# Expert blocks of 32 tokens on four column tiles, one store for a block, a second token buffer, and experts ordered by their counts

## The chip, the core and the metric

The kernel runs on one core of a Trainium2 chip. The metric is the device time of one execution in microseconds (us), the median of several runs. The engines named here are PE (TensorE: matmuls, and transposes, which are matmuls against an identity), DVE (VectorE), ACT (ScalarE), POOL (GpSimd) and SP (SyncE, which issues DMAs). ACT and POOL issue DMAs too. Each engine works through its own program in order; they meet through semaphores.

## The reference

One step of a streaming encoder layer with 640 tokens (512 of a prompt, 8 streams of 16) and width 1024, in float32. The change touches its second half, a mixture of 16 experts: a token chooses a group, and in it two experts.

```python
g_sel = jnp.argmax(g_logits, axis=-1)
...
top_v, top_i = lax.top_k(e_in, TOP_K_IN_GROUP)              # 2 of 4 experts of the group
w_sel = jax.nn.softmax(top_v, axis=-1) * g_w
e_ids = g_sel[:, None] * EXPERTS_PER_GROUP + top_i
combine = jnp.sum(jax.nn.one_hot(e_ids, N_EXPERTS) * w_sel[..., None], axis=1)
for e in range(N_EXPERTS):
    h = jax.nn.silu(xt @ lp['w1'][e]) * (xt @ lp['w3'][e])  # (640,1024) @ (1024,512), twice
    y = y + combine[:, e:e + 1] * (h @ lp['w2'][e])         # (640,512) @ (512,1024)
```

So there are 1280 pairs of token and expert. With the inputs of the reference the 16 experts receive 33, 33, 43, 55, 118, 271, 118, 361, 48, 42, 32, 22, 31, 25, 22 and 26 of them.

## The kernel before

The program runs the token mixer first (to about 804 us of the profile), then the routing on DVE and PE (to 819), then the **expert stage** (825.8 to 1160), then a stage that gathers each token's two results, adds them, normalises and stores (to the end).

**Blocks.** In the expert stage the pairs of an expert are cut into blocks of `SLOT` = 64 rows, so the 16 experts have 1, 1, 1, 1, 2, 5, 2, 6 and eight times 1 block, 27 in all, in the order of their numbers. The counts are known only on the chip: `ovc` holds each expert's blocks beyond the first, `ovp` where they start, and every engine reads both into registers (line 1661) at each expert. `each_block` (line 1658) is the loop that all engines share: one step for an expert's first block, whose "down" still belongs to the expert before, and an inner loop (line 1670) for its further blocks.

**A block on PE** (`step`, line 1774). A 64-row block uses half of PE's 128 columns, so two *column tiles* of 64 work side by side, on two halves of the output columns. The order is `up` half 0 (line 1750), `turn_hidden` of the block before (line 1758), `up` half 1, `turn_tokens` of the next block (line 1741), `down` of the block before (line 1769). An `up` half is 8 matmuls of 64 rows by 512 columns (w1 and w3 side by side), a `down` 8 as well. The trace records each of these float32 matmuls as two, so 8 stand there as 16.

**Around it.** POOL gathers the next block's 64 tokens from `xn_scratch` into `xg` with an indirect DMA (line 1716); a token is cut into two pieces, so that the 128 partitions are filled. PE turns `xg` (four transposes), DVE copies them from PSUM to `xe` (line 1832) and then makes the next gather's indices (`idx`, line 1826), on which POOL waits. ACT applies tanh (line 1812) and DVE makes the gated product `gg` in two operations (lines 1844, 1847); `turn_hidden` and a DVE copy give `hT`. After `down`, ACT copies the result from PSUM to `yb` (line 1800) and stores it to `block_outputs` in DRAM with two DMAs of 64 rows of 2 KB (line 1803). Ahead of the copy, ACT waits until the stores of the block before have landed (`y_stored`, line 1798), and PE's `down` waits for the copy of the block before (`y_ready`, line 1763).

**Weights.** An expert has 6 MiB: w1 and w3 in two halves of 2 MiB (rows of 2 KB), w2 of 2 MiB (rows of 4 KB). There are three buffers (`w`, `late` and `on`, in the profile's names). The first three experts' weights are loaded ahead, and SP refills a buffer (`refill`, line 1685) when the last block that reads its part is through: 13 refills.

**The routing** counts on DVE, by comparisons with tables: `over` (16 experts by 10 steps) gives the blocks of each expert, a scan their first rows, and `at_place`/`at_block` are the one-hot matrices from which PE makes the table of indices.

Of the kernel before, what the change touches and what calls it, by code (L numbers as in the profile page):

```python
# [8 lines left out]
I32 = mybir.dt.int32  # L9
# [27 lines left out]
SLOT = 64  # L37
# [5 lines left out]
CREDIT = 1  # L43
GELU_C = float(np.sqrt(2.0 / np.pi))
# [9 lines left out]
K_STEP = K_TOK + TT  # L54
K_PIECE = K_STEP + MAXOV + 1
K_KEEP = K_PIECE + 1
NK = K_KEEP


def shape_constants():  # L60

    c = np.zeros((P, NK + TT * NE), np.float32)
# [12 lines left out]
    c[:, K_STEP + 1:K_STEP + 1 + MAXOV] = SLOT * (1 + np.arange(MAXOV))  # L75
    c[:, K_KEEP:K_KEEP + TT * NE] = np.arange(TT * NE) % TT > 0
    c[:, K_PIECE] = p // SLOT
    c[:, K_DOWN:K_DOWN + 4] = 4 - np.arange(4)
    c[:, K_TOK:K_TOK + TT] = 2 * (p[:, None] + P * np.arange(TT))
    return c  # L80
# [960 lines left out]
def build_rest(nc, A, O, v):  # L1041
# [253 lines left out]
    ovp = sb("ovp", [1, NE + 1], I32)  # L1295
    idxt = sb("idxt", [P, NROWS])
    idx = sb("idx", [P, 1], I32)
    xg = sb("xg", [P, D // 2])
    sm = sb("sm", [P, TT, 16])
    xn2_pieces = xn2_d.rearrange("t (j c) -> (t j) c", j=2)  # L1300
# [56 lines left out]
    keep = sb("keep", [P, TT * NE], ctx=st4)  # L1357
# [5 lines left out]
    over = sb("over", [P, NE, MAXOV + 1], ctx=st4)  # L1363
    nblk = sb("nblk", [P, NE + 1], ctx=st4)
    rowst = sb("rowst", [P, NE + 1], ctx=st4)
# [18 lines left out]
    with nc.Block() as block:  # L1384
        @block.sync
        def _(sp_):
            for t in range(TT):
                if t == 2:
                    sp_.dma_start(wo[1], w_out[:, :, D // 2:]).then_inc(wo_in, 16)
                sp_.dma_start(x2[:, t, :], xp[:, t, :] if t < NQ else xs).then_inc(x2_in[t], 16)  # L1390
            sp_.dma_start(g2[:, :], A["norm2_g"].to_broadcast([P, D])).then_inc(r_in, 16)
            sp_.dma_start(keep[:, :], A["shape_constants"][:, K_KEEP:K_KEEP + TT * NE]).then_inc(r_in, 16)
# [116 lines left out]
        def _(dve):  # L1509
# [70 lines left out]
            nc.vector.tensor_tensor_scan(upto[:, :, :].rearrange("p e t -> p (e t)"), keep[:, :],  # L1580
# [10 lines left out]
            steps = cst[:, K_STEP:K_STEP + MAXOV + 1].rearrange("p (o j) -> p o j", o=1)  # L1591
            tt(over[:, :, :], bank[7][:, TT * NE:(TT + 1) * NE].rearrange("p (e o) -> p e o", o=1)
               .to_broadcast([P, NE, MAXOV + 1]), steps.to_broadcast([P, NE, MAXOV + 1]), ALU.is_gt)
            chain(nc.vector.tensor_reduce(nblk[:, 1:].rearrange("p (e o) -> p e o", o=1), over[:, :, :], AX.X, ALU.add))
            chain(nc.vector.tensor_tensor_scan(rowst[:, :], cst[:, K_ONE:K_ONE + NE + 1], nblk[:, :], 0.0,
                                               ALU.mult, ALU.add))

            rank, row, q, place, slotf = (pr[:, n, :, :] for n in range(5))
            tt(rk[:, :, :, :], oh[:, :, :, :], bank[7][:, 0:TT * NE].rearrange("p (o e t) -> p o t e", o=1, t=TT)
               .to_broadcast([P, 2, TT, NE]), ALU.mult)  # L1600
            nc.vector.tensor_tensor(rk2[:, :, :, :], oh[:, :, :, :], rowst[:, 0:NE].rearrange("p (o i e) -> p o i e", o=1, i=1)
# [8 lines left out]
            for n in range(2 * TT):  # L1610
                k, t = n // TT, n % TT
                nc.vector.tensor_scalar(
                    at_place[:, n, :].rearrange("p (j q) -> p j q", q=SLOT),
                    cst[:, K_RAMP:K_RAMP + SLOT].rearrange("p (o q) -> p o q", o=1).to_broadcast([P, P // SLOT, SLOT]),
                    pr[:, 3, k, t:t + 1], None, ALU.is_equal)
                nc.vector.tensor_scalar(at_block[:, n, :], cst[:, K_RAMP:K_RAMP + NROWS], pr[:, 1, k, t:t + 1],
                                        cst[:, K_TOK + t:K_TOK + t + 1], ALU.is_equal, ALU.mult).then_inc(hot_ready, 1)
            nc.vector.scalar_tensor_tensor(prev[:, :], cst[:, K_RAMP:K_RAMP + NE + 1], -1.0, rowst[:, :], ALU.mult, ALU.add)
# [28 lines left out]
    xt_done, xe_ready = sem("xt_done"), sem("xe_ready")  # L1647
# [34 lines left out]
    with nc.Block() as block:  # L1682
        @block.sync
        def _(sp_):
            def refill(e, buf):

                b = sp_.value_load(ovp[0:1, bass.ds(e - (NBUF - 1), 1)], min_val=0, max_val=OVMAX) + (e - (NBUF - 1))
                for half in range(2):
                    sp_.wait_ge(up_done[half], b)
                    load13(sp_, e, buf, half)  # L1690
                sp_.wait_ge(down_done, b + CREDIT)
                load2(sp_, e, buf)
# [42 lines left out]
        def _(pe):  # L1735
            def turn_tokens(b):
                pe.wait_ge(xg_in, b * 16 + 16)
                if not isinstance(b, int) or b > 0:
                    pe.wait_ge(xe_ready, b)
                for c in range(4):  # L1740
                    mm = nc.tensor.transpose(TOKB[:, c * P:(c + 1) * P], xg[:, c * P:(c + 1) * P], ident)
                mm.then_inc(xt_done, 1)

            def up(S, half):
                buf, n = S.up
                pe.wait_ge(w13_in[half][buf], n * UP_ARRIVED[half][buf])
                for c in range(4):
# [8 lines left out]
            def turn_hidden():  # L1756
                for c in range(2):
                    mm = nc.tensor.transpose(HIDB[:, c * P:(c + 1) * P], gg[:, c * P:(c + 1) * P], ident)  # L1758
                mm.then_inc(ht_done, 1)

            def down(S):
# [33 lines left out]
        def _(act):  # L1795
            def outputs(n, d):

                act.wait_ge(y_stored, n * 32 + (CREDIT - 32))
                act.wait_ge(down_done, d + CREDIT)
                nc.scalar.activation(yb[:, :], DNB[:, :], ACT.Copy).then_inc(y_ready, 1)  # L1800
                act.wait_ge(y_ready, n)
                for x in range(2):
                    act.dma_start(y_d[bass.ds((n - 1) * SLOT, SLOT), x * HD:(x + 1) * HD],
                                  yb[x * SLOT:(x + 1) * SLOT, :]).then_inc(y_stored, 16)
# [9 lines left out]
            def last(S):  # L1814
                outputs(S.b, S.b - 1)
                outputs(S.b + 1, S.b)
                act.wait_ge(y_stored, S.b * 32 + (CREDIT + 32))
# [5 lines left out]
        def _(dve):  # L1823
# [5 lines left out]
            def turned(b):  # L1829

                dve.wait_ge(xt_done, b + 1)
                nc.vector.tensor_copy(xe[:, :, :].rearrange("p c q -> p (c q)"), TOKB[:, :]).then_inc(xe_ready, 1)
                indices(b + 1)

            def hidden(S):
                dve.wait_ge(ht_done, S.b)
                nc.vector.tensor_copy(hT[:, :, :].rearrange("p c q -> p (c q)"), HIDB[:, 0:2 * P]).then_inc(ht_ready, 1)  # L1837

            def step(S):
                if S.down is not None:  # L1840
                    hidden(S)
                turned(S.b + 1)
# [109 lines left out]
```

## Time and profile before

| | us |
|---|---|
| median of 3 runs | 1200.76 (1199.95 to 1201.99) |
| the profiled execution, its own time | 1197.53 |
| its span in the trace | 1195.7 |
| expert stage in it, first `up` to last `down` | 825.8 to 1160.1 |

The span is what the trace covers. The profiled execution lies 0.27% under the median of the runs shown.

### The profile page before, as it was taken

Reading aid. Unit: us, or ns where it says so; the run is one execution under the profiler, and the core shown is the slowest. Engines: PE = TensorE matmul, PEld = TensorE weight load, DVE = VectorE, ACT = ScalarE, POOL = GpSimd, SP = SyncE. Lnnn points to the kernel's source line nnn. Section 1 sums busy time; section 2 is a strip of 40 time slices with the busy share of each in tenths; the row PEclk is TensorE's granted clock in tenths of the full one; section 3 lists DMA queues with packets and bytes.
Section 4 is the critical chain, followed back from the end, with each engine's and each line's share of the span. In section 5 each row is a group of like instructions: output and inputs, shape, how many; then the busy total and the mean of one; then the engine's idle time right before and its main releaser. Section 6 shows DMA issues by size and latency. Waiting matters only on the chain. (4 is left out here: it accounts for less than half of the span.)

```text
span 1195.7 us, 19605 instructions
## 1 busy us (share of the span) xinstructions
PE 1077.0 (90%) x6868; PEld 779.5 (65%) x6869; DVE 498.7 (42%) x979; ACT 266.6 (22%) x584; POOL 420.7 (35%) x461
## 2 busy tenths in 40 slices
PE   3999999999999995999979999986999999999760
PEld 3898888888898884999979994553333333332210
DVE  4448677786868678400051211224111111111106
ACT  4224243242525244311120001210000000000002
POOL 6466382745538300665546640000010110101013
PEclk9999999999999998999989999996999999999895
DMA  7353343242444200522362218917999573489977
GB/s 231 94 152 93 95 129 105 82 115 77 128 112 116 79 15 12 165 70 72 86 219 71 70 40 285 356 62 265 331 397 398 179 280 123 127 305 397 397 257 263
DMA packets 186539, 204.74 MB, mean 171 GB/s; under 512 B 13607, under 2 KB 132391, under 8 KB 186486
## 3 DMA queue, kind: packets, MB, share of 16 engines
q1 hardware_dynamic: 174790, 177.79, 45.0%
q10 hardware_dynamic: 7936, 13.37, 3.4%
q0 software_dynamic: 3760, 12.85, 3.1%
q8 instruction: 36, 0.59, 0.2%
q14 instruction: 17, 0.14, 0.0%
HBM read 180.84 MB, written 22.95 MB: 170 GB/s over the span
## 5 line engine op out<-in xcount | busy, mean ns | idle before, releaser
L178 POOL TENSOR_TENSOR wh<-raw,zcol 128x256 fp32r<-128x256 f32 x160 | 112.5, 703 | 173.4 <-DMA raw<-in_w_in 164.6
L1750 PE MATMUL bank<-w,xe 128*64 128x512 f32 x576 | 134.7, 611 | 12.2 <-DMA w<-in_w 9.6
L181 POOL TENSOR_TENSOR wl<-raw,wh 128x256 fp32r<-128x256 f32 x160 | 126.9, 793 | 12.6
L493 PE MATMUL bank<-xh,wh 128*128 128x320 f32 x384 | 122.3, 318 | 0.0
L494 PE MATMUL bank<-xl,wh 128*128 128x320 f32 x384 | 118.7, 309 | 0.0
L495 PE MATMUL bank<-xh,wl 128*128 128x320 f32 x384 | 118.7, 309 | 0.0
L1722 POOL TENSOR_TENSOR gate<-gate 128x1 f32<-128x1 f32 x27 | 5.2, 193 | 285.5 <-DVE idx L1826 282.8
L493 PE MATMUL bank<-wh,xh 128*128 128x256 f32 x320 | 93.6, 293 | 7.1 <-POOL wl L181 7.1
L1750 PEld LDWEIGHTS bank<-w,xe 128*64 128x64 f32 x576 | 40.4, 140 | 91.0 <-issue 78.0
L1153 POOL TENSOR_TENSOR w3h<-wraw,zcol 128x1024 fp32r<-128x1024 f32 x32 | 60.9, 1903 | 87.8 <-PE bank L1196 84.0
L494 PE MATMUL bank<-wl,xh 128*128 128x256 f32 x320 | 90.4, 283 | 0.0
L495 PE MATMUL bank<-wh,xl 128*128 128x256 f32 x320 | 90.4, 282 | 0.0
L1194 PE MATMUL bank<-bh,w3h 128*128 128x320 f32 x256 | 79.9, 312 | 6.1 <-DVE bl L1276 6.1
L1157 POOL TENSOR_TENSOR w3l<-wraw,w3h 128x1024 fp32r<-128x1024 f32 x32 | 80.9, 2529 | 2.5
L1837 DVE COPY hT<-bank 128x256 f32<-128x256 f32 x27 | 11.5, 424 | 165.5 <-PE bank L1758 165.5
L1195 PE MATMUL bank<-bl,w3h 128*128 128x320 f32 x256 | 79.6, 311 | 0.0
L1196 PE MATMUL bank<-bh,w3l 128*128 128x320 f32 x256 | 79.6, 311 | 0.0
L1194 PE MATMUL bank<-xh,w3h 128*128 128x320 f32 x256 | 79.1, 309 | 0.0
L493 PEld LDWEIGHTS bank<-xh,wh 128*128 128x128 f32 x384 | 72.1, 188 | 10.5 <-issue 10.5
L1196 PE MATMUL bank<-xh,w3l 128*128 128x320 f32 x256 | 79.0, 308 | 0.0
L1195 PE MATMUL bank<-xl,w3h 128*128 128x320 f32 x256 | 78.9, 308 | 0.0
L494 PEld LDWEIGHTS bank<-xl,wh 128*128 128x128 f32 x384 | 72.2, 188 | 0.2 <-issue 0.2
(273 smaller groups left out, 2076.5 us busy)
## 6 DMA issues: line engine op xcount, KB each, us to landing
w<-in_w SPq DMA_DIRECT2D x44, 1024.0 KB, 15.7
w<-in_w SPq DMA_DIRECT2D x11, 2048.0 KB, 17.7
raw<-in_w_in SPq DMA_DIRECT2D x38, 512.0 KB, 5.0
late<-in_w SPq DMA_DIRECT2D x10, 1024.0 KB
on<-in_w SPq DMA_DIRECT2D x5, 2048.0 KB, 15.5
kc<-in_cache_k SPq DMA_DIRECT2D x8, 1024.0 KB, 6.9
vc<-in_cache_v SPq DMA_DIRECT2D x8, 1024.0 KB, 6.1
wraw<-in_w_in SPq DMA_DIRECT2D x16, 512.0 KB, 4.0
```

The costliest lines, as they stand in the source:

```text
L178: nc.gpsimd.tensor_tensor(wh[:, k, j, :], r[:, k, :], zcol[:, 0:1].rearrange("p (a b) -> p a b", a=1) .to_broadcast([P, KT // PIECES, P]), ...
L181: ins = nc.gpsimd.tensor_tensor(wl[:, k, j, :], r[:, k, :], wh[:, k, j, :].bitcast(F32), ALU.subtract)
L493: nc.tensor.matmul(out, ah, bh, start=(k == 0), stop=False)
L494: nc.tensor.matmul(out, ah, bl, start=False, stop=False)
L495: mm = nc.tensor.matmul(out, al, bh, start=False, stop=(k == len(pairs) - 1))
L1153: nc.gpsimd.tensor_tensor(w3h[j][:, :, :], wraw[j][:, :, :], zcol3[:, 0:1].rearrange("p (a b) -> p a b", a=1).to_broadcast([P, KT, P]), AL ...
L1157: nc.gpsimd.tensor_tensor(w3l[j][:, :, :], wraw[j][:, :, :], w3h[j][:, :, :].bitcast(F32), ALU.subtract).then_inc(w3_split, 1)
L1194: nc.tensor.matmul(out, w3h[j][:, k, :], mh[:, k, c], start=(k == 0), stop=False)
L1195: nc.tensor.matmul(out, w3h[j][:, k, :], ml[:, k, c], start=False, stop=False)
L1196: mm = nc.tensor.matmul(out, w3l[j][:, k, :], mh[:, k, c], start=False, stop=(k == KT - 1))
L1750: mm = nc.tensor.matmul(UPB[j * SLOT:(j + 1) * SLOT, :], xe[:, c, half * SLOT:(half + 1) * SLOT], up_rows(buf, k, k + 1)[:, 0, :, j * HF:( ...
L1837: nc.vector.tensor_copy(hT[:, :, :].rearrange("p c q -> p (c q)"), HIDB[:, 0:2 * P]).then_inc(ht_ready, 1)
```

## The change

Blocks have `SLOT` = 32 rows, so the experts have 2, 2, 2, 2, 4, 9, 4, 12, 2, 2 and six times 1 block, 47 in all. PE works in four column tiles of 32: an `up` half and a `down` are 16 matmuls of 32 rows by 256 columns. A token is cut into four pieces of 256, `xg` is 128 x 256, `turn_tokens` has two transposes and `turn_hidden` one.

The gathered tokens go from `xg` to a second buffer, `xs`, by a DVE copy (`staged`) that stands ahead of the copy of the turned tokens; the indices for the next gather, and that gather, no longer wait for the transposes but for this copy.

A block's result leaves `yb` (128 partitions of 256) in one DMA: its DRAM side is written as 4 pieces by 32 rows by 256 columns, its SBUF side as 128 partitions.

The experts come in another order: `FIXED` = 3 stay first, the others are ranked by their counts and `SPREAD` says which rank comes at which turn. By the counts above the experts come as 0, 1, 2, 7, 14, 11, 5, 13, 15, 4, 12, 10, 6, 9, 8, 3, with 2, 2, 2, 12, 1, 1, 9, 1, 1, 4, 1, 1, 4, 2, 2, 2 blocks. DVE makes that order in the routing, and SP reads from a table (`turn_of`) which expert's weights to load.

```diff
-SLOT = 64
+SLOT = 32
+NP = P // SLOT
...
+FIXED = 3
+SPREAD = (0, 1, 2, 3, 15, 14, 4, 13, 12, 5, 11, 10, 6, 9, 8, 7)
...
+    c[:, K_KEY:K_KEY + NE] = np.where(e < FIXED, 4096.0 * (FIXED - e), -e / 32.0)
+    c[:, K_RANK:K_RANK + NE] = SPREAD
...
+            tt(key[:, :], counts, late_k[:, K_KEY - NK:K_RANK - NK], ALU.add)
+            tt(larger[:, :, :], key[:, :].rearrange("p (o e) -> p o e", o=1).to_broadcast(pairs),
+               key[:, :].rearrange("p (e o) -> p e o", o=1).to_broadcast(pairs), ALU.is_gt)
+            nc.vector.tensor_reduce(rank_e[:, :].rearrange("p (e o) -> p e o", o=1), larger[:, :, :], AX.X, ALU.add)
...
+            tt(at_turn[:, :, :], rank_e[:, :].rearrange("p (o e) -> p o e", o=1).to_broadcast(pairs),
+               late_k[:, K_RANK - NK:NK4 - NK].rearrange("p (i o) -> p i o", o=1).to_broadcast(pairs), ALU.is_equal)
...
                 b = sp_.value_load(ovp[0:1, bass.ds(e - (NBUF - 1), 1)], min_val=0, max_val=OVMAX) + (e - (NBUF - 1))
+                x = sp_.value_load(turn_of[0:1, bass.ds(e, 1)], min_val=0, max_val=NE - 1)
                 for half in range(2):
                     sp_.wait_ge(up_done[half], b)
-                    load13(sp_, e, buf, half)
+                    load13(sp_, x, buf, half)
...
             def gather(b):
-                if not isinstance(b, int) or b > 0:
-                    pool.wait_ge(xt_done, b)
+                pool.wait_ge(xs_ready, b)
                 pool.wait_ge(idx_in, b + 1)
...
-                for c in range(4):
-                    k = half * 4 + c
-                    for j in range(2):
-                        mm = nc.tensor.matmul(UPB[j * SLOT:(j + 1) * SLOT, :],
-                                              xe[:, c, half * SLOT:(half + 1) * SLOT],
+                for k in range(half * KT // 2, (half + 1) * KT // 2):
+                    x, c = k // XC, k % XC
+                    for j in range(NP):
+                        mm = nc.tensor.matmul(UPB[j * SLOT:(j + 1) * SLOT, 0:2 * HF],
+                                              xe[:, c, x * SLOT:(x + 1) * SLOT],
                                               up_rows(buf, k, k + 1)[:, 0, :, j * HF:(j + 1) * HF],
                                               start=(k == 0), stop=(k == KT - 1))
...
-                act.wait_ge(y_stored, n * 32 + (CREDIT - 32))
+                act.wait_ge(y_stored, n * 16 + (CREDIT - 16))
                 act.wait_ge(down_done, d + CREDIT)
-                nc.scalar.activation(yb[:, :], DNB[:, :], ACT.Copy).then_inc(y_ready, 1)
+                nc.scalar.activation(yb[:, :], DNB[:, 0:HD], ACT.Copy).then_inc(y_ready, 1)
                 act.wait_ge(y_ready, n)
-                for x in range(2):
-                    act.dma_start(y_d[bass.ds((n - 1) * SLOT, SLOT), x * HD:(x + 1) * HD],
-                                  yb[x * SLOT:(x + 1) * SLOT, :]).then_inc(y_stored, 16)
+                act.dma_start(y_d[bass.ds((n - 1) * SLOT, SLOT), :].rearrange("s (x c) -> x s c", x=NP), yb[:, :]) \
+                    .then_inc(y_stored, 16)
...
+            def staged(b):
+
+                dve.wait_ge(xg_in, b * 16 + 16)
+                if not isinstance(b, int) or b > 0:
+                    dve.wait_ge(xt_done, b)
+                nc.vector.tensor_copy(xs[:, :], xg[:, :]).then_inc(xs_ready, 1)
                 indices(b + 1)
...
                 if S.down is not None:
                     hidden(S)
+                staged(S.b + 1)
                 turned(S.b + 1)
```

The first piece of the program's order is PE's, before the change, from an expert's first block (whose `down` reads `w_1`) into the inner loop; REGISTER_ALU, TENSOR_LOAD, ISA and the branches are work of PE's sequencer.

```order
L1750 MATMUL bank<-late,xe 64x512 x8
L1737 ISA
L1741 MATMUL bank<-cst,xg 128x128 x4
L1769 MATMUL bank<-w_1,hT 64x512 x8
L1661 REGISTER_ALU
L1661 TENSOR_LOAD ovc
L1661 ISA x2
L1669 COMPARE_AND_BRANCH
L1661 TENSOR_LOAD ovp
```

The same place of PE's program after the change:

```order
L1788 MATMUL bank<-late,xe 32x256 x16
L1775 REGISTER_ALU
L1779 MATMUL bank<-cst,xs 128x128 x2
L1804 MATMUL bank<-w_1,hT 32x256 x16
L1699 REGISTER_ALU
L1699 TENSOR_LOAD ovc
L1699 ISA x2
L1707 COMPARE_AND_BRANCH
L1699 TENSOR_LOAD ovp
```

The register work stands in the same place with the same rows, behind a `down` of 16 small matmuls instead of 8 large ones. The second place is ACT's inner loop; before the change (the brackets name the semaphores that an instruction waits for):

```order
L1800 ACTIVATE yb<-bank 128x512 [waits down_done,y_stored]
L1803 ISA [waits y_ready]
L1803 DMA block_outputs<-yb 64x512
L1803 ISA
L1803 DMA block_outputs<-yb 64x512
L1809 REGISTER_ALU
L1812 ACTIVATE th<-bank 128x256 [waits s_ready,up_done1]
```

And after it:

```order
L1835 ACTIVATE yb<-bank 128x256 [waits down_done,y_stored]
L1837 ISA [waits y_ready]
L1837 DMA block_outputs<-yb 4x32x256
L1843 REGISTER_ALU
L1846 ACTIVATE th<-bank 128x128 [waits s_ready,up_done1]
```

One DMA whose outermost count is 4 has taken the place of two whose outermost count is 64; the copy still waits for the store before it, and the tanh stands behind both. The third place is DVE's inner loop after the change:

```order
L1878 COPY hT<-bank 128x128 [waits ht_done]
L1870 ISA
L1873 COPY xs<-xg 128x256 [waits xt_done,xg_in]
L1860 ISA
L1860 TENSOR_SCALAR idx<-idxt 128x1
L1865 REGISTER_ALU
L1866 COPY xe<-bank 128x256 [waits xt_done]
L1886 SCALAR_TENSOR_TENSOR gg<-th,bank 128x128 [waits th_ready]
L1889 SCALAR_TENSOR_TENSOR gg<-gg,bank 128x128 [waits s_ready]
```

Before, DVE had no copy from `xg` and made `idx` behind the copy to `xe`; the wait for the gather (`xg_in`) has moved from PE's transposes to DVE, ahead of `xe` and `gg`.

## Rows read from the trace of the kernel before

**Rows 1.** Stretches: length, busy PE, PEld, DVE, ACT, POOL, PE clock, DMA share, GB/s

```profile
826.00:1160.00 334.00, 317.06 (x1458) 105.80 (x1458) 52.78 (x140) 26.46 (x54) 32.09 (x55) 0.99 0.79 290
...
1104.00:1117.00 13.00, 9.74 (x34) 2.88 (x34) 0.42 (x1) 0.00 (x0) 0.00 (x0) 0.74 1.04 398
```

**Rows 2.** Timeline of one block of 64 tokens, PE and ACT

```profile
883.53 0.60 ACT L1800 ACTIVATE yb<-bank 128x512 f32<-128x512 f32 x1 [3.85 <-PE bank L1769]
...
887.15 3.65 PE L1750 MATMUL bank<-w,xe 128*64 128x512 f32 x16
...
890.74 0.66 PE L1741 MATMUL bank<-cst,xg 128*128 128x128 f32 x4
...
891.33 3.65 PE L1769 MATMUL bank<-w,hT 128*64 128x512 f32 x16
...
895.09 0.60 ACT L1800 ACTIVATE yb<-bank 128x512 f32<-128x512 f32 x1 [3.85 <-PE bank L1769]
...
895.86 1.19 ACTq L1803 DMA_DIRECT2D block_outputs<-yb  x2
```

**Rows 3.** Timeline of TensorE, an attention line on four column tiles

```profile
57.00 1.07 PE L582 MATMUL bank<-kc,qbd 128*32 128x256 f32 x16 [0.44 <-ACT kc L713]
```

**Rows 4.** Line 1661 between two one-block experts, 1052.5 to 1055.6

```profile
L1661 PEldq TENSOR_LOAD <-ovc x1: 307/307/307, 1053.2 to 1053.2; - x1
...
L1661 PEldq TENSOR_LOAD <-ovp x1: 305/305/305, 1054.3 to 1054.3; - x1
```

**Rows 5.** Line 1746 in the same stretch

```profile
L1746 PEldq FUSED_REGOPS  x1: 37/37/37, 1055.2 to 1055.2; - x1
```

**Rows 6.** Timeline of TensorE in that stretch

```profile
1053.12 3.65 PE L1769 MATMUL bank<-w,hT 128*64 128x512 f32 x16
```

**Rows 7.** Waits of TensorE in the stage: total, times, longest

```profile
PE bank L1750 <- DMA w<-in_w: 9.6, 4, 4.0
PE bank L1750 <- DMA late<-in_w: 4.9, 2, 2.6
```

**Rows 8.** Timeline of TensorE after its longest wait

```profile
1107.26 6.16 PE L1750 MATMUL bank<-w,xe 128*64 128x512 f32 x16 [3.99 <-DMA w<-in_w]
```

**Rows 9.** Timeline of SyncE's DMA issues, w2 of four late refills

```profile
1083.29 2.56 SPq L1338 DMA_DIRECT2D w<-in_w  x1
...
1134.92 2.47 SPq L1338 DMA_DIRECT2D w<-in_w  x1
```

**Rows 10.** All stores of the stage, issue to landing

```profile
DMA to landing us min/median/max: 2.3/5.4/7.4
```

**Rows 11.** Packets, MB, share of 16 engines by queue, 872.7 to 878.3

```profile
q1 hardware_dynamic: 723, 1.67, 78.2%
q10 hardware_dynamic: 144, 0.25, 12.0%
```

**Rows 12.** DMA traffic of line 1138's stores, 699.2 to 701.2

```profile
DMA packets 60, 0.15 MB, mean 74 GB/s; under 512 B 24, under 2 KB 24, under 8 KB 60
...
out_new_conv_sample<-srow SPq DMA_DIRECT2D x1, 96.0 KB
```

**Rows 13.** Gathers into xg, issue to landing

```profile
DMA to landing us min/median/max: 3.0/6.0/7.8
```

**Rows 14.** Timeline of VectorE in the routing

```profile
811.38 0.32 DVE L1513 TENSOR_TENSOR rk<-oh,bank 128x160 f32<-128x160 f32 x1
811.74 0.32 DVE L1601 TENSOR_TENSOR rk<-oh,rowst 128x160 f32<-128x160 f32 x1
...
818.67 0.26 DVE L1624 TENSOR_SCALAR idxt<-bank,cst 128x38 f32<-128x38 f32 x1 [0.49 <-PE bank L1468]
```

**Rows 15.** Timeline of TensorE at the stage's first block

```profile
825.82 8.67 PE L1750 MATMUL bank<-w,xe 128*64 128x512 f32 x32 [0.78 <-DVE xe L1832]
```

**Rows 16.** Timeline at the stage's end

```profile
1161.00 1.13 ACTq L1803 DMA_DIRECT2D block_outputs<-yb  x2
1163.94 0.20 ACT L1818 ACTIVATE gate<-eps_t 128x1 f32<-128x1 f32 x1 [3.12 <-DMA block_outputs<-yb]
```

More of the change, by code:

```diff
@@ L53 @@
 K_ID, K_ONE, K_UPTO, K_SEL, K_M0, K_M1, K_RAMP, K_DOWN, K_TOK = (0, 128, 256, 384, 448, 449, 450, 578, 582)
[L54 to L57, printed above, removed]
+K_PIECE = K_TOK + TT
+NK = K_PIECE + 1
+K_KEEP = NK
+K_STEP = K_KEEP + TT * NE
+K_KEY = K_STEP + MAXOV + 1
+K_RANK = K_KEY + NE
+NK4 = K_RANK + NE
 def shape_constants():
-    c = np.zeros((P, NK + TT * NE), np.float32)
+    c = np.zeros((P, NK4), np.float32)
     p = np.arange(P)
@@ L1356, in build_rest @@
     gap = sb("gap", [P, TT, NG], ctx=st4)
-    keep = sb("keep", [P, TT * NE], ctx=st4)
+    late_k = sb("late_k", [P, NK4 - NK], ctx=st4)
+    keep = late_k[:, 0:TT * NE]
     oh = sb("oh", [P, 2, TT, NE], ctx=st4)
@@ L1362, in build_rest @@
     rk2 = sb("rk2", [P, 2, TT, NE], ctx=st4)
-    over = sb("over", [P, NE, MAXOV + 1], ctx=st4)
+    over = x2T[:, 4:, :].rearrange("p k q -> p (k q)")[:, 0:NE * (MAXOV + 1)].rearrange("p (e o) -> p e o", e=NE)
     nblk = sb("nblk", [P, NE + 1], ctx=st4)
+    nblk_e = sb("nblk_e", [P, NE], ctx=st4)
+    key = sb("key", [P, NE], ctx=st4)
+    larger, at_turn = (x2T[:, 2 * i:2 * i + 2, :].rearrange("p k q -> p (k q)").rearrange("p (a b) -> p a b", b=NE)
+                       for i in range(2))
+    rank_e = sb("rank_e", [P, NE], ctx=st4)
+    rowst_e = sb("rowst_e", [P, NE], ctx=st4)
+    who = sb("who", [P, NE], ctx=st4)
     rowst = sb("rowst", [P, NE + 1], ctx=st4)
@@ L1391, in _ @@
             sp_.dma_start(g2[:, :], A["norm2_g"].to_broadcast([P, D])).then_inc(r_in, 16)
-            sp_.dma_start(keep[:, :], A["shape_constants"][:, K_KEEP:K_KEEP + TT * NE]).then_inc(r_in, 16)
+            sp_.dma_start(late_k[:, :], A["shape_constants"][:, NK:NK4]).then_inc(r_in, 16)
             sp_.dma_start(wr[:, :, 0:NG], A["w_group"][0].rearrange("(k p) n -> p k n", p=P)).then_inc(r_in, 16)
@@ L1579, in _ @@
             dve.wait_ge(oh_ready, 1)
-            nc.vector.tensor_tensor_scan(upto[:, :, :].rearrange("p e t -> p (e t)"), keep[:, :],
+            nc.vector.tensor_tensor_scan(upto[:, :, :].rearrange("p e t -> p (e t)"), keep,
                                          both[:, :, :].rearrange("p e t -> p (e t)"), 0.0, ALU.mult, ALU.add) \
@@ L1590, in _ @@
             dve.wait_ge(ranks_done, 1)
-            steps = cst[:, K_STEP:K_STEP + MAXOV + 1].rearrange("p (o j) -> p o j", o=1)
+            steps = late_k[:, K_STEP - NK:K_KEY - NK].rearrange("p (o j) -> p o j", o=1)
+            counts = bank[7][:, TT * NE:(TT + 1) * NE]
+            pairs = [P, NE, NE]
+            tt(key[:, :], counts, late_k[:, K_KEY - NK:K_RANK - NK], ALU.add)
+            tt(larger[:, :, :], key[:, :].rearrange("p (o e) -> p o e", o=1).to_broadcast(pairs),
+               key[:, :].rearrange("p (e o) -> p e o", o=1).to_broadcast(pairs), ALU.is_gt)
+            nc.vector.tensor_reduce(rank_e[:, :].rearrange("p (e o) -> p e o", o=1), larger[:, :, :], AX.X, ALU.add)
             tt(over[:, :, :], bank[7][:, TT * NE:(TT + 1) * NE].rearrange("p (e o) -> p e o", o=1)
                .to_broadcast([P, NE, MAXOV + 1]), steps.to_broadcast([P, NE, MAXOV + 1]), ALU.is_gt)
-            chain(nc.vector.tensor_reduce(nblk[:, 1:].rearrange("p (e o) -> p e o", o=1), over[:, :, :], AX.X, ALU.add))
+            nc.vector.tensor_reduce(nblk_e[:, :].rearrange("p (e o) -> p e o", o=1), over[:, :, :], AX.X, ALU.add)
+            tt(at_turn[:, :, :], rank_e[:, :].rearrange("p (o e) -> p o e", o=1).to_broadcast(pairs),
+               late_k[:, K_RANK - NK:NK4 - NK].rearrange("p (i o) -> p i o", o=1).to_broadcast(pairs), ALU.is_equal)
+            tt(larger[:, :, :], at_turn[:, :, :], nblk_e[:, :].rearrange("p (o e) -> p o e", o=1).to_broadcast(pairs),
+               ALU.mult)
+            chain(nc.vector.tensor_reduce(nblk[:, 1:].rearrange("p (i o) -> p i o", o=1), larger[:, :, :], AX.X, ALU.add))
             chain(nc.vector.tensor_tensor_scan(rowst[:, :], cst[:, K_ONE:K_ONE + NE + 1], nblk[:, :], 0.0,
                                                ALU.mult, ALU.add))
+            tt(larger[:, :, :], at_turn[:, :, :].rearrange("p i e -> p e i"),
+               rowst[:, 0:NE].rearrange("p (o i) -> p o i", o=1).to_broadcast(pairs), ALU.mult)
+            nc.vector.tensor_reduce(rowst_e[:, :].rearrange("p (e o) -> p e o", o=1), larger[:, :, :], AX.X, ALU.add)
             rank, row, q, place, slotf = (pr[:, n, :, :] for n in range(5))
@@ L1617, in _ @@
                                         cst[:, K_TOK + t:K_TOK + t + 1], ALU.is_equal, ALU.mult).then_inc(hot_ready, 1)
+            tt(larger[:, :, :], at_turn[:, :, :],
+               cst[:, K_RAMP:K_RAMP + NE].rearrange("p (o e) -> p o e", o=1).to_broadcast(pairs), ALU.mult)
+            chain(nc.vector.tensor_reduce(who[:, :].rearrange("p (i o) -> p i o", o=1), larger[:, :, :], AX.X, ALU.add))
+            nc.vector.tensor_copy(turn_of[:, :], who[0:1, :])
             nc.vector.scalar_tensor_tensor(prev[:, :], cst[:, K_RAMP:K_RAMP + NE + 1], -1.0, rowst[:, :], ALU.mult, ALU.add)
@@ L1736, in turn_tokens @@
             def turn_tokens(b):
-                pe.wait_ge(xg_in, b * 16 + 16)
+                pe.wait_ge(xs_ready, b + 1)
                 if not isinstance(b, int) or b > 0:
                     pe.wait_ge(xe_ready, b)
-                for c in range(4):
-                    mm = nc.tensor.transpose(TOKB[:, c * P:(c + 1) * P], xg[:, c * P:(c + 1) * P], ident)
+                for c in range(XC):
+                    mm = nc.tensor.transpose(TOKB[:, c * P:(c + 1) * P], xs[:, c * P:(c + 1) * P], ident)
                 mm.then_inc(xt_done, 1)
@@ L1756, in turn_hidden @@
             def turn_hidden():
-                for c in range(2):
-                    mm = nc.tensor.transpose(HIDB[:, c * P:(c + 1) * P], gg[:, c * P:(c + 1) * P], ident)
-                mm.then_inc(ht_done, 1)
+                nc.tensor.transpose(HIDB[:, 0:P], gg[:, :], ident).then_inc(ht_done, 1)
             def down(S):
@@ L1766, in down @@
                 for k in range(DNC):
-                    j, c = k // 2, k % 2
-                    for x in range(2):
-                        mm = nc.tensor.matmul(DNB[x * SLOT:(x + 1) * SLOT, :], hT[:, c, j * SLOT:(j + 1) * SLOT],
+                    for x in range(NP):
+                        mm = nc.tensor.matmul(DNB[x * SLOT:(x + 1) * SLOT, 0:HD], hT[:, k * SLOT:(k + 1) * SLOT],
                                               w2b[buf][:, k, x * HD:(x + 1) * HD],
```

32 lines of the change are left out of this document (17 added, 15 removed).

## The prediction

> **What bounds it now.** I read the stretches first: of the 334.00 us of the expert stage PE is busy 317.06, at a granted clock of 0.99 [rows 1]. So this stage goes at PE's pace, and the timeline of a block shows the pace: an `up` half at 887.15, the token transposes at 890.74 and `down` at 891.33 follow one another without a wait, and ACT's copies to `yb`, one a block, start at 883.53 and 895.09, 11.56 us apart [rows 2]. An `up` half, eight pairs of column tiles, takes 3.59 to the next piece: 0.43 a pair and 0.15 of transition. 24 pairs are 10.3 us of a block, the transitions 1.25. The list of waits shows where PE stands still: 9.6 + 4.9 = 14.5 us, all for weights, at the end of the stage [rows 7]. After the longest of these waits, 3.99 us, an `up` half took 6.16 instead of 3.65 [rows 8], and the granted clock of that stretch is 0.74 [rows 1]: 2.5 us more. ACT, DVE, POOL and the stores are hidden today: the loaded landing of a store, 5.4 us in the median [rows 10], fits into a block of 11.56. That cover is what I watch, because the change halves it.
>
> **Matmuls on four column tiles.** 256 columns instead of 512 make a step of four tiles 0.43/2 = 0.215 us. The nearest row agrees: 16 recorded matmuls of 128 x 256 on tiles of 32, four steps, took 1.07 us with the last one's tail [rows 3], where two tiles at a time would need eight steps, 1.7. A block is then 24 x 0.215 = 5.17, plus transitions of 0.90 (three transposes fewer): 6.07. 47 blocks are 285.3 us, against 27 x 11.556 = 312.0 today: **-26.7**.
>
> **Register work between experts.** At 1053 to 1055, between two one-block experts, PE's sequencer reads `ovc` at 1053.2 and `ovp` at 1054.3 (0.31 each) [rows 4] and comes to the next `up` at 1055.2 [rows 5], 2.1 us after the first of it. `down` had begun at 1053.12 [rows 6]: the sequencer pushes `down`'s 16 pairs and runs ahead of them, so today 3.5 us of matmuls hide the 2.1. After the change the same 16 pairs are half a `down`, about 0.86 us. I charge the difference, 1.3 us, at six one-block experts (7.8). Entering an inner loop has three register loads, some 0.6 more: 1.9 at ten experts (19); leaving one has one load: 0.5 to 1.05 at nine (6.7). Together **+33.5**. Bounds: 12 if the queue holds all 32 pairs of the new `down`, 45 if it holds fewer than 16.
>
> **Weights.** The late waits come from eight one-block experts in a row, for which 11.56 us do not cover a refill: `w2` refills are issued at 1083.29 and, three later, at 1134.92, 17.2 us each [rows 9]. In the new order the blocks of 12, 9, 4 and 4 stand between groups of small experts. I keep 4 of the 17 (14.5 + 2.5): **-13**.
>
> **Routing.** `over` doubles to 320 elements, and nine operations of up to 256 elements are new ahead of the one-hot matrices or behind them. Operations of 160 elements start 0.36 apart (811.38, 811.74), so I take 0.45 for 256; the 0.49 that DVE waits before `idxt` hides a part [rows 14]: +4.2. At the first block the copy to `xs` adds 0.4; two transposes fewer and a smaller `xe` copy give 0.8 back. First `up` at 829.6 instead of 825.82 [rows 15]: **+3.8**.
>
> **Gather.** It may start earlier, but must land within a 6.07 us block; it takes 3.0 to 7.8, 6.0 in the median [rows 13]. With 0.9 of copy and issue around it, it binds only in inner loops under loads: +2 (0 to 5), in the 4 kept above. The wait stands on DVE now: behind it are `idx`, `xe` and `gg`, and PE's transposes and next `up` wait for those.
>
> **The store.** Two issues become one, which saves ACT some 0.6 a block, hidden either way; at the very end the second issue and half the copy fall away, -0.85. But the shape of the one DMA changes how many DMA engines carry it. The state stores of line 1138 show how: they have 3, 24, 1 and 8 rows, and their traffic is 60 packets, 36 rows and 24 small completion writes [rows 12]. 24 is 3 + 12 + 1 + 8: not 16 for the 24-row store, but 12, the largest number up to 16 that divides its outermost count. Today's 64 rows give 16 engines with four 2 KB rows each. The new store is 128 partitions on one side and 4 pieces x 32 x 256 on the other. No store before has two sides that differ, but to be cut alike on both by the outermost count it has four parts: four engines with 32 rows of 1 KB each. The Trainium skill, page "DMA: Bandwidth & Descriptors", section "Why a DMA increments its semaphore by 16 and not by 1", states the rule for both patterns, which would be four here; the 24 writes agree for equal sides, and no run here shows unequal ones.
>
> Its price: while a store landed under loads, 128 store rows took 12.0% of 16 engines over 5.6 us, 84 ns each, and 723 packets of the weights' queue 78.2%, 97 ns each [rows 11]. A 1 KB row is 42 ns, and one weight row comes between two store rows: 28 further rows x 0.139 = 3.9, on top of 5.4: landing after 9.3 us. Bounds: 6.6 if the rows go without alternating (28 x 0.042), 11.3 behind 4 KB weight rows (28 x 0.210). Idle: 2.3 + 1.2 = 3.5.
>
> ACT's next copy waits for that landing, behind it stands the tanh, and PE's `down` waits for the copy. A block under loads then takes 0.38 (copy) + 0.17 (895.69 to the issue at 895.86 [rows 2]) + 9.3 + 0.1 = 9.95, instead of 6.07 + 33.5/47 = 6.78: 3.2 more. Loads last 13 x 17.2 = 224 us, and the four engines carry 24 KB more a block, at 393 KB per 17.2 us another 1.05: n = (224 + 1.05 n)/9.95, n = 25. I take 22, since a store issued near a load's end lands in a quiet DMA: 22 x 3.2 = **+70**. The waits kept above hide behind it, -3.
>
> **The sum.** The stage ends today at 1160.1: 825.8 + 312.0 + 1.4 (first halves at a low clock, 8.67 [rows 15]) + 17 + 3.3 (first and last block's helpers) = 1159.5. After: 829.6 + 285.3 + 1.5 + 33.5 + 4 + 2 = 1156; with the four-engine store 1156 + 67 = 1223. From stage end to the finished execution is 1197.5 - 1160.1 = 37.4; the last store costs 1.2 more landing less 0.85 (today 1161.00 to 1163.94 [rows 16]). 1223 + 37.4 + 0.3 = 1261 in the profiled execution's time; the median of the runs stood 3.2 above that: **1264 us**, 5% slower.
>
> **The rivals.**
> - *The store runs on 16 engines* (the 128 partitions decide). It then lands within 5.4 to 6.1, hidden, and the sum is 1156 + 37.4 - 0.85 = 1192.6, median **1196**: faster. The change decides for gain where a store lands in under about 6 us.
> - *The same, and PE's queue holds the whole `down`.* Register stalls 12 instead of 33.5: about **1176**. Against it: the sequencer goes on just when `down`'s first matmul starts [rows 4, 6], so the rows show it 16 pairs ahead, not 32.
> - *Four engines, rows not alternating.* Landing 6.6, period 7.25, 0.5 more for 31 blocks: **1212**.
> - *Four engines and the clock falls.* The 3.9 us that PE waits per block come in one piece at `down`, as long as the 3.99 that took the clock away. A half-clock block is up to 12.1 us, 2.2 above the period: +48 at most, **1310**. For it: the one case of [rows 8]; against it: the 2.5 us of a slower half disappear in the same slack, and the clock would have to stay down through all loaded blocks.
> - *Column tiles of 32 do not overlap* would cost hundreds of us; the attention line excludes it.
>
> **Numbers.** Four engines as worked out, 1225 to 1303: 0.56; with a lost clock above that, 0.06; without alternation, 1200 to 1225: 0.14. Sixteen engines: 0.24, of which a third at 1176 to 1187. A difference of 0.2% (2.4 us) is about what the runs can tell from none. Faster 0.20, same 0.05, slower 0.75. The range 1192 to 1303 leaves out some 0.13 below and 0.06 above; four engines alone, 1205 to 1303.
>
> **What would show it.** The landing of `block_outputs`: about 9 us under loads and 3.5 idle, or 5.4 and 2.3 if wrong; DMA traffic of a lone store with four completion writes, not 16; ACT's `yb` copies waiting for `block_outputs`, PE's `down` for `yb`, blocks of 10 us under loads and 6.1 without. Steps of PE: four tiles every 0.215; sequencer gaps of 1 to 2 us between experts and none inside loops; weight waits under 4 us in all; `idxt` 4 us later. Short landings with PE busy throughout would make the prediction wrong.

## The result, and the profile after

The changed kernel takes 1241.98 us (median of 4 runs, 1240.91 to 1245.09) against 1201.38 for the kernel before (4 runs): a ratio of 1.0335, interval 1.0314 to 1.0356. It is slower by 3.4%; forecast were 1264 us and 5%. Its profiled execution took 1242.42, its span is 1240.7.

The stretch of the expert stage, in the columns of [rows 1]:

```profile
829.90:1204.00 374.10, 311.30 (x4654) 160.02 (x4653) 73.12 (x289) 31.11 (x94) 55.07 (x95) 0.94 0.69 254
```

The stage lasts from 830.5 to 1203.4: 372.9 us, where it was 334.3. PE is busy for 311 of it, hardly less than before, and the mean granted clock is 0.94 instead of 0.99. The lists of waits say where the rest goes. First PE (total, times, longest), then ACT; "issue" stands for a gap in which the engine waited for nothing that the profile shows. Line 1788 is an `up` half, 1804 `down`, 1779 the token transposes, 1835 the copy to `yb`, 1846 the tanh, 1889 the end of `gg`, 1873 the copy to `xs`:

```profile
PE bank L1804 <- ACT yb L1835: 46.2, 23, 3.3
PE bank L1788 <- DVE gg L1889: 7.6, 10, 1.3
PE bank L1788 <- issue: 7.6, 12, 1.3
PE bank L1779 <- DVE xs L1873: 3.7, 1, 3.7
...
```

```profile
ACT yb L1835 <- DMA block_outputs<-yb: 193.7, 28, 8.4
ACT th L1846 <- PE bank L1788: 98.4, 24, 24.4
ACT yb L1835 <- PE bank L1804: 36.4, 18, 2.1
...
```

The 3.7 us for `xs` lie ahead of the first `up`. No wait for weights is left; the 14.5 us of [rows 7] are gone. In their place `down` (line 1804) waits 46.2 us for the copy to `yb`, 23 times, and that copy stood still for 193.7 us because the store ahead of it had not landed. The timeline of ACT and PE in a stretch with weight loads shows one turn of it:

```profile
853.71 0.39 ACT L1835 ACTIVATE yb<-bank 128x256 f32<-128x256 f32 x1 [5.64 <-DMA block_outputs<-yb]
854.29 1.06 ACTq L1837 DMA_DIRECT2D block_outputs<-yb  x1
...
864.20 0.38 ACT L1835 ACTIVATE yb<-bank 128x256 f32<-128x256 f32 x1 [8.35 <-DMA block_outputs<-yb]
...
864.63 3.59 PE L1804 MATMUL bank<-w,hT 128*32 128x256 f32 x32 [2.64 <-ACT yb L1835]
864.76 1.05 ACTq L1837 DMA_DIRECT2D block_outputs<-yb  x1
...
873.27 0.38 ACT L1835 ACTIVATE yb<-bank 128x256 f32<-128x256 f32 x1 [7.00 <-DMA block_outputs<-yb]
...
873.71 1.93 PE L1804 MATMUL bank<-on,hT 128*32 128x256 f32 x32 [1.08 <-ACT yb L1835]
```

The copy at 853.71 is stored from 854.29 on; the next copy starts at 864.20, as soon as that store has landed, 9.9 us after its issue, and the one after that at 873.27, 8.5 after the issue at 864.76. The copies were 11.56 us apart for 64 rows [rows 2]; here they are 9 to 10.5 apart for 32. After the wait of 2.64 us one `down` took 3.59 us instead of 1.93; the stretch of that `down` and the next `up` half, in the columns of [rows 1]:

```profile
864.60:868.20 3.60, 3.57 (x32) 1.41 (x33) 0.57 (x2) 0.28 (x1) 0.00 (x0) 0.53 1.04 383
868.20:870.10 1.90, 1.90 (x37) 1.13 (x33) 0.00 (x0) 0.00 (x0) 0.00 (x0) 1.00 0.98 344
```

The granted clock is 0.53 in the first, about the lower of its two levels (1.2 instead of 2.4 GHz), and 1.00 in the second. Between the weight loads the same program does what its matmuls allow:

```profile
1024.01 0.39 ACT L1835 ACTIVATE yb<-bank 128x256 f32<-128x256 f32 x1 [2.02 <-PE bank L1804]
1024.57 0.56 ACTq L1837 DMA_DIRECT2D block_outputs<-yb  x1
...
1030.09 0.38 ACT L1835 ACTIVATE yb<-bank 128x256 f32<-128x256 f32 x1 [2.02 <-PE bank L1804]
```

Copies are 6.08 us apart there, and ACT waits for PE, no longer for the DMA. The last store lands in an otherwise quiet DMA, so its traffic can be counted as in [rows 12]:

```profile
DMA packets 132, 0.13 MB, mean 41 GB/s; under 512 B 4, under 2 KB 132, under 8 KB 132
...
q10 hardware_dynamic: 132, 0.13, 13.8%
...
block_outputs<-yb ACTq DMA_DIRECT2D x1, 128.0 KB
```

132 packets are 128 rows of 1 KB and 4 completion writes: four DMA engines. The same count at the end of the kernel before:

```profile
DMA packets 160, 0.26 MB, mean 90 GB/s; under 512 B 32, under 2 KB 32, under 8 KB 160
```

Its two stores together have 160 packets, 128 rows and 32 writes, 16 for each.

### The profile page after: what moved, and what is told of

The parts are those of the page before. It is cut to its first block and busy times, and to the rows that moved or that the text cites. A ratio compares the mean times of both kernels' runs of the same rounds, so it can differ in the third digit from the quotient of the medians.

```text
span 1240.7 us, 27023 instructions
## 1 busy us (share of the span) xinstructions
PE 1070.9 (86%) x10061; PEld 833.0 (67%) x10062; DVE 520.9 (42%) x1138; ACT 271.5 (22%) x624; POOL 442.7 (36%) x501
## 5 line engine op out<-in xcount | busy, mean ns | idle before, releaser
L1788 PE MATMUL bank<-w,xe 128*32 128x256 f32 x2560 | 159.4, 391 | 13.9 <-DVE gg L1889 7.0
L1788 PEld LDWEIGHTS bank<-w,xe 128*32 128x32 f32 x2560 | 81.3, 112 | 76.1 <-issue 29.7
L1804 PE MATMUL bank<-w,hT 128*32 128x256 f32 x1280 | 87.5, 420 | 35.4 <-ACT yb L1835 35.3
L1760 POOL TENSOR_TENSOR gate<-gate 128x1 f32<-128x1 f32 x47 | 9.1, 193 | 292.3 <-DVE idx L1860 290.5
L1804 PEld LDWEIGHTS bank<-w,hT 128*32 128x32 f32 x1280 | 41.3, 119 | 68.6 <-issue 42.4
L502 PEld LDWEIGHTS bank<-xh,wh 128*128 128x128 f32 x384 | 72.0, 188 | 10.5 <-issue 10.2
```

The costliest lines, as they stand in the source:

```text
L502: nc.tensor.matmul(out, ah, bh, start=(k == 0), stop=False)
L1788: mm = nc.tensor.matmul(UPB[j * SLOT:(j + 1) * SLOT, 0:2 * HF], xe[:, c, x * SLOT:(x + 1) * SLOT], up_rows(buf, k, k + 1)[:, 0, :, j * HF: ...
L1804: mm = nc.tensor.matmul(DNB[x * SLOT:(x + 1) * SLOT, 0:HD], hT[:, k * SLOT:(k + 1) * SLOT], w2b[buf][:, k, x * HD:(x + 1) * HD], start=(k ...
```

## The experiments

All times are medians, and the ratios, with 95% intervals, are to the kernel before in runs on the same chip. The theory was that the one store runs on four engines, that it lands late under weight loads, and that ACT's wait for it sets the pace; the main rivals were the register work between experts, blocks of 32 rows as such, and the load that the stores put on four engines.

| kernel | us | ratio (interval) |
|---|---|---|
| the change | 1241.98 | 1.0335 (1.0314 to 1.0356) |
| `two_engines`: the store as two, on two engines | 1307.91 | 1.0874 (1.0836 to 1.0912) |
| `before_one_store`: before, its two stores as one | 1281.60 | 1.0681 (1.0640 to 1.0722) |
| `own_order`: the change, experts by number | 1249.13 | 1.0401 (1.0373 to 1.0429) |
| `four_stores`: the change with four stores a block | 1196.22 | 0.9953 (0.9936 to 0.9970) |
| `four_own_order`: that, experts by number | 1218.78 | 1.0140 (1.0119 to 1.0160) |
| `four_one_buffer`: that, without the second token buffer | 1206.19 | 1.0032 (1.0016 to 1.0048) |
| `four_reads`: that, register reads moved | 1191.90 | 0.9916 (0.9899 to 0.9933) |
| `two_buffers`: the change, two result buffers | 1207.22 | 1.0047 (1.0030 to 1.0065) |
| `two_buffers_reads`: that, register reads moved | 1207.71 | 1.0051 (1.0030 to 1.0072) |
| `before_order`: before, with the order alone | 1186.14 | 0.9872 (0.9850 to 0.9894) |

**Four stores.** One store for each piece of 32 rows, as the two stores before.

```diff
...
-                act.dma_start(y_d[bass.ds((n - 1) * SLOT, SLOT), :].rearrange("s (x c) -> x s c", x=NP), yb[:, :]) \
-                    .then_inc(y_stored, 16)
+                for x in range(NP):
+                    act.dma_start(y_d[bass.ds((n - 1) * SLOT, SLOT), x * HD:(x + 1) * HD],
+                                  yb[x * SLOT:(x + 1) * SLOT, :]).then_inc(y_stored, 16)
```

> The changed kernel with its one store cut into four again, one for each 32 rows of 1 KB. Theory (the single store runs on four DMA engines, and the next copy waits for its landing): both sides of each DMA are 32 rows, so 16 engines carry it; landing under loads 5 to 6 us, ACT's wait for it small, the 46.2 us that PE waits for the copies and most of the 14 us at a low clock behind them go: 1242 - 55 = about 1185 us, 1178 to 1195. Rival (32-row blocks as such are too short for any store under loads, or the four issues of 0.5 us each load ACT): PE keeps at least half of its waits, 1215 or more.

1196.22 us, 46 less than the change. The DMA traffic of one block's four stores, and PE's waits in the stage:

```profile
DMA packets 192, 0.13 MB, mean 35 GB/s; under 512 B 64, under 2 KB 192, under 8 KB 192
```

```profile
PE bank L1788 <- issue: 12.6, 16, 1.3
PE bank L1788 <- DVE gg L1890: 8.3, 7, 1.8
PE bank L1788 <- DMA w<-in_w: 6.9, 2, 3.9
PE bank L1779 <- DVE xs L1874: 6.4, 7, 3.7
...
PE bank L1804 <- ACT yb L1835: 0.4, 1, 0.4
```

128 rows now have 64 completion writes, four times 16. PE's wait for the copies has shrunk from 46.2 us to 0.4. The theory holds; the size expected was 11 us too good, and the time lies just outside its range, because other waits come up behind it: for weights (6.9 after none), ahead of `up` with no cause shown (12.6 after 7.6), and for the second token buffer (2.7 of the 6.4; the other 3.7 lie ahead of the first `up`, as in the change). The prediction's first rival had 1196 for just this case, though its terms for the weights and the register work were others.

**More rows on fewer engines.** The store as two DMAs of 2 pieces by 32 rows each, and, on the kernel before, its two stores joined into one of 2 pieces by 64 rows:

```diff
...
+                for h in range(2):
+                    act.dma_start(y_d[bass.ds((n - 1) * SLOT, SLOT), h * 2 * HD:(h + 1) * 2 * HD]
+                                  .rearrange("s (x c) -> x s c", x=2),
+                                  yb[h * 2 * SLOT:(h + 1) * 2 * SLOT, :]).then_inc(y_stored, 16)
```

> The changed kernel with its store cut into two DMAs of 2 pieces by 32 rows. Theory: each runs on two engines, and both on the same two, so these carry 64 rows each instead of 32; 32 more rows at 0.2 us under loads are 6.4 us: landing 15 to 16, blocks under loads 16.5, some 14 to 16 of them: 1290 to 1320 us. Rival (the number of engines is not what makes the landing long): two issues instead of one cost at most 0.5 us a block on ACT: 1242 to 1255.

```diff
-                for x in range(2):
-                    act.dma_start(y_d[bass.ds((n - 1) * SLOT, SLOT), x * HD:(x + 1) * HD],
-                                  yb[x * SLOT:(x + 1) * SLOT, :]).then_inc(y_stored, 16)
+                act.dma_start(y_d[bass.ds((n - 1) * SLOT, SLOT), :].rearrange("s (x c) -> x s c", x=2), yb[:, :]) \
+                    .then_inc(y_stored, 16)
```

> The kernel before with nothing changed but its two stores joined into one DMA of 2 pieces by 64 rows of 2 KB. Theory: two engines with 64 rows each, at 0.084 + 0.097 us a row under loads 11.6 us on top of 4: landing about 16, longer than its block of 11.56: some 14 blocks under loads cost 5 us more, 1255 to 1290 us. Rival (a block of 64 rows covers it, or one issue less helps): 1196 to 1204.

1307.91 and 1281.60 us, both inside what the theory gave and far from the rivals. The waits of PE and ACT in the first, then ACT's and the last store's traffic in the second:

```profile
PE bank L1804 <- ACT yb L1835: 95.4, 19, 8.9
```

```profile
ACT yb L1835 <- DMA block_outputs<-yb: 243.2, 32, 13.8
```

```profile
ACT yb L1800 <- DMA block_outputs<-yb: 224.9, 20, 16.7
```

```profile
DMA packets 130, 0.26 MB, mean 32 GB/s; under 512 B 2, under 2 KB 2, under 8 KB 130
```

With half the engines PE's wait doubles (46.2 to 95.4 us), and ACT's longest wait goes from 8.4 to 13.8 us. That the two stores of a block share the same two engines is read from this, not counted. In the joined store, with 64 rows of 2 KB an engine, it is 16.7, where the kernel before had no such wait; of the 80 us that this kernel is slower, PE's waits for the copy are 35.1 (35.7 after 0.6), its waits for weights 16.1 (30.6 after 14.5), and matmuls at a low clock some 18. Without weight loads the last store lands 3.3 us after its issue in the change, 5.0 in `two_engines`, and 7.9 joined. The joined store has 128 rows and 2 completion writes: the outermost count of its DRAM side is 2. So the smaller of the two sides' counts decides, in both kernels, and no block size is needed to make it costly.

**The wait or the load.** The one store stays, but `yb` has two halves with a semaphore each, so a copy waits for the store before the last.

```diff
+                def put(i):
+                    act.wait_ge(y_stored[i], (n + i) * 8)
...
+                with act.If(n % 2 == 0):
+                    put(0)
+                with act.Else():
+                    put(1)
```

> The changed kernel, its one store on four engines left as it is, with two result buffers and a semaphore for each (ACT branches on the block's parity): a copy waits for the store before the last. Theory (the price is the wait for the landing, 8 to 10 us against a block of 6.1): two blocks of 6.1 cover it, PE's 46 us of waits for copies and the 14 us of low clock go: 1185 to 1200 us. Rival (the price is the load on four DMA engines: store rows hold up the weights' rows there): weights come late instead, 1210 to 1235.

1207.22 us: 35 us of the 46 come back, 11 do not. The expectation was missed on its upper side, and the rival's on its lower. ACT's copies never wait for a store now, PE's waits are others; behind them the landing of `w2`, issue to landing, in the saturated stretch 1040 to 1140, here and with four stores:

```profile
PE bank L1789 <- issue: 15.6, 18, 1.3
PE bank L1789 <- DMA w<-in_w: 14.3, 3, 8.8
...
PE bank L1789 <- DMA late<-in_w: 3.3, 1, 3.3
```

```profile
DMA to landing us min/median/max: 18.6/19.4/21.1
```

```profile
DMA to landing us min/median/max: 17.5/17.6/18.2
```

A `w2` load needs 19.4 us instead of 17.6, and PE waits 14.3 + 3.3 us for weights instead of 6.9. So three quarters of the loss was the wait. For the last quarter the 10.7 us more of waits for weights speak for the load on four engines, which the wait had hidden as long as it held the blocks up; no run takes that load away alone, and the branch on the block's parity, which is new here, may have a part in it ("issue" 15.6 after 12.6).

**Register reads.** An expert's three reads are moved into its first block's step, on PE behind the hidden transpose, the second `up` half and the token transposes, first on the kernel with four stores (there on ACT too, behind its store), then on the one with two buffers.

```diff
+                S.read()
                 up(S, 1)
+                S.read()
                 turn_tokens(S.b + 1)
+                S.read()
```

> The kernel with four stores a block, and on PE and ACT an expert's three register reads moved from behind its first block's step into it (PE: behind the hidden transpose, behind the second up half, behind the token transposes). Theory (the 27 us that PE stands still between a down and the next up, beyond 0.2 a block, are mostly the sequencer reading registers with only about 16 pairs ahead): 10 to 16 of them go, 1180 to 1187 us. Rival (the tanh, late behind four store issues, ends these gaps): 1192 to 1198.

> The same with PE's register reads moved into the first block's step. Theory: with one store issue instead of four the tanh is not late, so more of the register gaps is kept than the 4 us which the kernel with four stores gave: 6 to 12 us below the kernel with two buffers, 1175 to 1192. Rival (the gathers and weights take up what the reads give): within 4 us of it.

1191.90 us, 4 less than the kernel with four stores and just under the rival's range, and 1207.71, no gain, as the rival had it. PE's waits with four stores:

```profile
PE bank L1788 <- DVE xs L1888: 9.2, 11, 3.7
PE bank L1797 <- DVE gg L1904: 6.0, 6, 2.3
PE bank L1797 <- DMA w<-in_w: 5.9, 2, 4.3
PE bank L1813 <- issue: 5.2, 12, 0.6
PE bank L1797 <- issue: 1.0, 4, 0.3
...
```

The gaps ahead of `up` with no other cause ("issue") have gone from 12.6 to 1.0 us, so the register reads did make them. But 5.2 of it comes back ahead of `down`, and the gathers take more (9.2 after 6.4). With two buffers "issue" goes from 15.6 to 5.6 us (4.5 of it ahead of `down`), the waits for the gathered tokens inside the stage from 5.4 to 13.5, and those for weights stay (17.6 and 17.7). Both expectations of a large gain were wrong: what is freed runs into the gather.

**The order of the experts.** With the tables set to the order of the numbers, once with the one store and once with four:

```diff
-FIXED = 3
-SPREAD = (0, 1, 2, 3, 15, 14, 4, 13, 12, 5, 11, 10, 6, 9, 8, 7)
+FIXED = NE
+SPREAD = tuple(range(NE))
```

> The changed kernel with the experts in the order of their numbers (the tables alone differ; the routing's operations stay). Theory of the order: six one-block experts stand together at the end, each needs 17 to 18 us for its weights and some 10 us for its block, so PE waits 5 to 8 us for weights six times: 1270 to 1290 us. Rival (the order is worth nothing while the stores set the pace): 1240 to 1250.

> The kernel with four stores a block and the experts in the order of their numbers. Theory of the order: the six one-block experts at the end need about 17 us of weights each and have 7.5 us of work; part of the loads runs ahead, some 20 to 35 us of waits are left: 1212 to 1232 us. Rival (with short blocks the loads are the bound in any order): 1193 to 1202.

1249.13 and 1218.78 us. The order is worth 7 us in the change and 23 us with four stores. Of PE's waits in the first:

```profile
PE bank L1804 <- ACT yb L1835: 30.8, 16, 3.3
PE bank L1788 <- DMA w<-in_w: 11.4, 4, 5.4
PE bank L1788 <- DMA late<-in_w: 8.8, 2, 6.4
```

And for weights in the second:

```profile
PE bank L1788 <- DMA w<-in_w: 19.3, 5, 7.3
...
PE bank L1788 <- DMA late<-in_w: 8.8, 2, 7.1
```

28.1 us, against 6.9 in the new order. With one store the first expectation was too high, and its rival's range held: PE waits 20.2 us for weights there, but its waits for the copy are 30.8 us instead of 46.2. Then the order alone, on the kernel before (of the change's diff the tables, the routing, `turn_of` and SP's read of it):

```diff
 SLOT = 64
+NP = P // SLOT
...
+FIXED = 3
+SPREAD = (0, 1, 2, 3, 15, 14, 4, 13, 12, 5, 11, 10, 6, 9, 8, 7)
...
+                x = sp_.value_load(turn_of[0:1, bass.ds(e, 1)], min_val=0, max_val=NE - 1)
```

> The kernel before with the new order of the experts alone: blocks of 64 rows, two stores, one token buffer as they were. Theory (the order spreads the large experts, so PE's 14.5 us of weight waits and the 2.5 us of low clock go, but for some 3 us; the new routing operations cost 3.7): 1202 - 17 + 3 + 3.7, 1187 to 1195 us. Rival (runs of two one-block experts at 11.6 us against 17.2 us of weights still wait, and the routing eats the rest): 1198 to 1206.

1186.14 us, the fastest of all, 1 below the range expected. All waits that the list has for PE (the first lies ahead of the stage's first `up`):

```profile
PE bank L1779 <- PEq L1402: 3.9, 1, 3.9
PE bank L1788 <- DVE gg L1885: 1.9, 1, 1.9
PE bank L1788 <- DVE xe L1870: 0.8, 1, 0.8
PE bank L1807 <- ACT yb L1838: 0.6, 1, 0.6
```

Not one for weights; the stage is 317.5 us long, 16.8 less than before, which is the 14.5 + 2.5 us of [rows 7, 8].

**The second token buffer.** With four stores, PE turns `xg` itself again, and the indices come behind `xe`.

```diff
-                pe.wait_ge(xs_ready, b + 1)
+                pe.wait_ge(xg_in, b * 16 + 16)
...
-                staged(S.b + 1)
                 turned(S.b + 1)
+                staged(S.b + 1)
```

> The kernel with four stores a block and without the second token buffer: PE turns the gathered tokens from where they land, as before. Theory: the next gather starts 1.6 us behind the token transposes instead of 0.4 ahead, needs 5.6 us under loads and a block lasts 6.1: 1 to 1.5 us more in each loaded block that stands in a loop, none without loads: 1208 to 1230 us. Rival (the gather hides in a block either way): 1193 to 1198.

1206.19 us: 10 more than with four stores, a little less than the theory gave (12 was its least) and far from the rival. PE's wait for the gather:

```profile
PE bank L1780 <- DMA xg<-xn_scratch,idx: 20.6, 17, 2.9
```

20.6 us where it was 2.7 inside the stage with the buffer. A block of 6.1 us needs the buffer.

## Why the prediction came out as it did

**The direction and its cause were right.** The store's engines follow the outermost counts of both sides: four writes in 132 packets, two in the joined store of the kernel before. ACT's wait for the landing and PE's wait behind it are what the change cost; taking them away gives 46 us back (four stores), doubling the rows on each engine costs 66 more, 49 of it in waits and 18 in matmuls at a low clock. The Trainium skill, page "DMA: Bandwidth & Descriptors", section "Why a DMA increments its semaphore by 16 and not by 1", takes the largest number up to 16 that divides both counts; 4, 2 and 16 are what the traces show.

**The block:** 6.07 us forecast, 6.08 measured between loads.

**The store's price** was 67 us; in the profile it is 46.2 of waits and 15.8 of matmuls at a low clock (added up over all `up` halves and `down`s as the time beyond 1.93 each), 62. The landing of 9.3 us was right (8.4 to 9.9 in 24 of ACT's 28 waits; 3.3 for the last store, without loads, where 3.5 was forecast), and so was the number of blocks: 22 forecast, 23 waits. The loss of the clock was a rival there, with a chance of 0.06; in fact it came in part: after some waits of 1.8 to 3.3 us a `down` went at the lower clock, and the clock was back one to four pieces later. Other waits as long left it alone:

```profile
1081.72 1.93 PE L1804 MATMUL bank<-w,hT 128*32 128x256 f32 x32 [2.98 <-ACT yb L1835]
...
1147.66 3.43 PE L1804 MATMUL bank<-w,hT 128*32 128x256 f32 x32 [1.80 <-ACT yb L1835]
```

A loaded block lasted as long as its store's landing and 0.57 us more, whether its `down` was slow or not: the next copy came 9.07 us later after the slow `down` at 864.63, and 8.94 later after the fast one at 1081.72. So a slow `down` took up time that PE would have waited, which is what the prediction held against this rival.

**Register work** was mis-sized: 33.5 us forecast, some 20.3 in the profile (by how much the gaps from `down` to `up` exceed those inside a loop, the waits for `gg` among them; four of these, 2.1 us, stand where no register is read, behind a tanh that comes late after the store, and belong to the store). The step that failed is the 16 pairs of lead. At a one-block expert after the change PE's sequencer reads the first register while `down` has only just begun, and PE then stands still for 0.68 us, not 1.3 (the last row ends with the window):

```profile
L1699 PEldq TENSOR_LOAD <-ovc x1: 300/300/300, 1047.3 to 1047.3; - x1
...
L1699 PEldq TENSOR_LOAD <-ovp x1: 309/309/309, 1048.4 to 1048.4; - x1
```

```profile
1046.77 1.93 PE L1804 MATMUL bank<-w,hT 128*32 128x256 f32 x32
1049.39 0.85 PE L1788 MATMUL bank<-late,xe 128*32 128x256 f32 x12 [0.68 <-issue]
```

`down` starts at 1046.77 and the read at 1047.3: about ten of the 32 pairs are through, so the sequencer is some 22 ahead. The bounds (12 to 45) held it.

**Weights:** 4 us kept, none left in the change, 6.9 with four stores, when the stores no longer held the blocks up. **Routing:** +4.2 forecast; `idxt` starts at 824.27, 5.6 later than in [rows 14], of which 1.3 were there before the routing began (its first operation at 805.65 instead of 804.31): 4.3. **Gather:** 2 forecast, nothing inside the stage in the change, 2.7 with four stores.

**The sum.** The stage ends at 1203.4 instead of the forecast 1223: 13 us of the difference are the registers, 5 the store's price, about 3 the weights and the gather, less a start 0.9 later. From there to the end of the profiled execution it was 39.0 us instead of 37.7, and the median stood 0.4 below that execution, where the prediction had added 3.2. The time was in the range, on the favourable side of the likeliest case.

What stays open: which waits cost the clock. One of 2.98 us did not and one of 1.80 did, in the same kernel, and no run varies this alone.

## What to carry to other kernels

Joining several stores into one saves issues, but look at both access patterns first: here the number of DMA engines went by the outermost counts, and a pattern that began with 2 or 4 pieces put all rows on 2 or 4 engines; count the completion writes of a lone store to see it. When blocks are made shorter, list everything that the old block's length covered (landings, gathers, register reads, weight loads) and compare each with the new length. And try the parts of a change alone: here the order of the experts is worth 1.3% by itself, while the smaller blocks, for all their faster matmuls, use their gain up in gaps.

## What the runs showed that was not expected

- One store issue on ACT took 1.05 us on four engines under weight loads, 0.55 without loads.
- A short wait can cost the clock: after 2.64 us of waiting a `down` took 3.59 instead of 1.93 us in the changed kernel, while another kept its clock after 2.98 us. The runs do not say what tells these apart.
- Beside stores on four engines the weight loads were slower too: 19.4 us for `w2` with two result buffers, 17.6 with four stores on 16 engines.
